# A two-layer trunk with a mixture of experts on one core: block pairs without tokens move to the front of the block table, and the first tokens are fetched ahead of the scatter

## The reference, condensed

```python
def hierarchical_moe(h, wg, bg, we, be, w1, w3, w2):
    x = h.reshape(b * t, d)
    pg_sel, g_sel = lax.top_k(softmax(x @ wg + bg), 1)          # one of 4 groups
    le = (x @ we + be).reshape(-1, N_GROUPS, EXPERTS_PER_GROUP)
    w_top, i_top = lax.top_k(softmax(le_sel), TOP_K)            # two of its 4 experts
    ...
    hid = silu(x @ w1[e]) * (x @ w3[e])
    y = sum over the two experts of gate * (hid @ w2[e])
```

## Time and profile before

| | |
|---|---|
| median of 3 runs | 2230.29 us (2224.9 to 2230.62) |
| profiled execution: its time / its span | 2219.47 us / 2217.3 us |
| busy: PE, DVE, ACT, POOL | 1915.4, 896.2, 481.3, 373.1 us |
| mean granted TensorE clock | 0.918 of 2.4 GHz |
| pair loop, layer 0 (first L986 to last DVE copy) | 893.9 to 1083.7 us |
| pair loop, layer 1 | 1941.5 to 2149.4 us |

### The profile page before, as it was taken

The page is one execution under the profiler, slowest core; times in us unless marked ns, Lnnn a source line. Parts: engine busy times, 40 slices in busy tenths (PEclk is TensorE's granted clock), DMA queues, the critical chain, the costliest instruction groups (busy, mean ns, idle before and its releaser), DMA issues. The chain is left out here.

```text
span 2217.3 us, 24642 instructions
## 1 busy us (share of the span) xinstructions
PE 1915.4 (86%) x9669; PEld 1300.0 (59%) x9669; DVE 896.2 (40%) x1686; ACT 481.3 (22%) x810; POOL 373.1 (17%) x280
## 2 busy tenths in 40 slices
PE   3899978978888895899679999888888889599975
PEld 2455655558888754444345566556888865444433
DVE  2179014565555424011237920546555541311114
ACT  1211013351111213122131101344111120322212
POOL 0001150043433102100111000005444300300001
PEclk8999897999999997899789999899999999699996
DMA  9322896800000003999562112530000000499953
GB/s 358 41 75 82 278 290 209 298 1 1 1 1 1 10 2 129 354 364 365 218 161 76 38 57 77 197 126 1 1 1 1 1 12 0 168 383 358 372 226 121
DMA packets 113920, 302.54 MB, mean 136 GB/s; under 512 B 27904, under 2 KB 35746, under 8 KB 100642
## 3 DMA queue, kind: packets, MB, share of 16 engines
q1 hardware_dynamic: 65424, 218.73, 26.7%
q0 software_dynamic: 14080, 53.48, 7.3%
q10 hardware_dynamic: 34322, 28.99, 4.6%
HBM read 235.09 MB, written 67.05 MB: 136 GB/s over the span
## 5 line engine op out<-in xcount | busy, mean ns | idle before, releaser
L626 PE MATMUL ps<-hreg,ring 128*128 128x512 f32 x768 | 400.2, 603 | 7.7 <-ACT hreg L1141 7.7
L627 PEld LDWEIGHTS ps<-hreg,ring 128*128 128x128 f32 x768 | 147.8, 192 | 187.6 <-issue 187.6
L986 PE MATMUL ps<-ring,tok 128*128 128x512 f32 x544 | 237.9, 595 | 0.2 <-issue 0.2
L986 PEld LDWEIGHTS ps<-ring,tok 128*128 128x128 f32 x544 | 103.9, 191 | 130.9 <-issue 130.9
L627 PE MATMUL ps<-hreg,ring 128*128 128x128 f32 x768 | 149.0, 276 | 0.0
L1969 POOL TENSOR_TENSOR hreg<-hreg,cst 128x512 f32<-128x512 f32 x70 | 88.9, 1270 | 301.7 <-DVE hreg L1674 254.7
L1001 PE MATMUL ps<-ring,work 128*128 128x512 f32 x272 | 123.7, 598 | 0.0
L626 PEld LDWEIGHTS ps<-hreg,ring 128*128 128x128 f32 x768 | 118.8, 195 | 8.0 <-issue 8.0
L1881 DVE TENSOR_TENSOR work<-work,ps 128x256 f32<-128x256 f32 x34 | 14.2, 421 | 252.5 <-ACT work L1364 252.5
L1503 DVE SCALAR_TENSOR_TENSOR mixA<-cin_reg,small,mixA 128x655 f32<-128x655 f32 x120 | 107.0, 895 | 0.0
L1687 DVE TENSOR_TENSOR hreg<-hreg,ps 128x512 f32<-128x512 f32 x50 | 34.3, 687 | 164.9 <-PE ps L846 164.9
(11 more groups left out here) (358 smaller groups left out, 3306.5 us busy)
## 6 DMA issues: line engine op xcount, KB each, us to landing
ring<-in_w SPq DMA_DIRECT2D x102, 1024.0 KB, 8.2
ring<-in_w_mod SPq DMA_DIRECT2D x24, 2048.0 KB, 8.6
ring<-in_w_in SPq DMA_DIRECT2D x12, 2048.0 KB, 9.0
ys<-zs ACTq DMA_DIRECT2D x34, 512.0 KB, 7.8
tok<-xs SPq DMA_DIRECT2D x30, 512.0 KB, 11.0
xs<-zero POOLq DMA_DIRECT2D x8, 1792.0 KB, 19.6
ys<-zero POOLq DMA_DIRECT2D x8, 1664.0 KB, 18.6
ring<-in_w_out SPq DMA_DIRECT2D x4, 2048.0 KB, 8.1
```

Source lines behind the costliest of these rows:

```text
L626: mm(o[:, 0:TS], lhs(k), rhs(k)[:, 0:TS], start=k == 0, stop=k == nk - 1)
L627: ins = mm(o[:, TS:T], lhs(k), rhs(k)[:, TS:T], start=k == 0, stop=k == nk - 1)
L986: ins = mm(bank(2 + q), xgT[q][:, k, :], w, start=k == 0, stop=k == KD - 1)
```

## The change

The diff makes seven edits. On POOL the fetches for blocks 2 and 3 move ahead of the ten scatters. On PE the second `turn_block` writes another part of PSUM (columns 2048 on) and no longer waits for ACT's first copy; ACT copies from there. SP waits for the second fetch (`xf_loaded[1]`) before it starts the weights of block 1. The bias matmuls L939 are gone: two small matmuls in the output projection (m == 2) spread the bias row over partitions, DVE keeps it in `crb`, and adds it where it copied the logits. DVE norms rows 0 to 3 right after `lrow`, POOL rows 4 to 7, and ACT takes the rows in order; DVE's late `norm_one(1)` after the routing is gone. Unused pairs come first: `skip` (unused blocks) is added to the block numbers, `skip` times 128 to `slots`, and `blocks` gets three more entries; slots are written later on DVE, behind the hot rows. And the branch of each loop turns round: pairs below `unused` only raise counters. Not shown below: the ACT and DVE loops, which turn round as PE's does, with the same counters raised as before, and declarations.

```diff
@@ -516,15 +517,22 @@
                     need(ht_copied, c_ + 1)
                     sp.dma_start(hx[P * c_:P * (c_ + 1), :], htok[:, c_, :]).then_inc(hx_stored.sem, 16)
                 need(blocks_ready, 1)
+                need(xf_loaded[1], 16)
                 sp.sem_inc(once["turns"], 1)
-                e = sp.value_load(blocks[0:1, 1:2], min_val=0, max_val=NE - 1)
+                e = sp.value_load(blocks[0:1, NBLK + 2:NBLK + 3], min_val=0, max_val=NE - 1)
                 up_load(1, e)
                 down_load(1, e)
                 need(xs_written, 16 * 2 * NCH)
-                in_use = sp.value_load(blocks[0:1, NBLK:NBLK + 1], min_val=1, max_val=NBLK)
+                unused = sp.value_load(blocks[0:1, NBLK + 1:NBLK + 2], min_val=2, max_val=NBLK + 2)
                 experts = {}
                 with sp.Fori(1, NPAIR) as pr:
-                    with sp.If(pr * 2 < in_use):
+                    with sp.If(pr * 2 < unused):
+                        for q in range(2):
+                            sp.sem_inc(ring_loaded[q], 32)
+                            sp.sem_inc(w2_loaded[q].sem, 16)
+                            sp.sem_inc(xg_loaded[q].sem, 16)
+                    with sp.Else():
+
                         for q in range(2):
                             e = sp.value_load(blocks[0:1, bass.ds(pr * 2 + q, 1)], min_val=0, max_val=NE - 1)
                             experts[q] = e
@@ -536,15 +544,6 @@
                             xg_load(q, pr * 2 + q + 2)
                             sp.wait_ge(y_done.sem, y_done.at(l, q - 1) + pr * 2)
                             down_load(q, experts[q])
-                    with sp.Else():
-
-                        for q in range(2):
-                            sp.wait_ge(ring_loaded[q], up_base[l][q] + pr * 32)
-                            sp.sem_inc(ring_loaded[q], 32)
-                            sp.wait_ge(w2_loaded[q].sem, w2_loaded[q].at(l, 0) + pr * 16)
-                            sp.sem_inc(w2_loaded[q].sem, 16)
-                            sp.wait_ge(xg_loaded[q].sem, xg_loaded[q].at(l, -16) + pr * 16)
-                            sp.sem_inc(xg_loaded[q].sem, 16)
 
             sp.wait_ge(once["y_stored"], 32)
 
...
@@ -916,6 +915,12 @@
                         for k in range(KD):
                             ins = mm(ps[0:2, 2900:2920], mod[:, 24 + k, :], wr[:, k, :], start=k == 0, stop=k == KD - 1)
                         ins.then_inc(logit_rows.sem, 1)
+                    if m == 2:
+                        need(logit_copied, 1)
+                        for g_ in range(2):
+                            ins = mm(ps[:, 2940 + 20 * g_:2960 + 20 * g_], ident[0:2, g_:g_ + 1].to_broadcast([2, P]), crow,
+                                     start=True, stop=True)
+                        ins.then_inc(logit_rows.sem, 1)
 
                 need(mod2_ready, 2)
@@ -934,9 +939,7 @@
                 need(route_loaded, 16)
                 for t in range(NCH):
                     o = ps[:, 2048 + 20 * t:2068 + 20 * t]
-                    g_ = 0 if t < TS // P else 1
-                    mm(o, lrow[:, P * t:P * (t + 1)], route_c[:, X_SEL:X_SEL + 20], start=True, stop=False)
-                    ins = mm(o, ident[0:2, g_:g_ + 1].to_broadcast([2, P]), crow, start=False, stop=True)
+                    ins = mm(o, lrow[:, P * t:P * (t + 1)], route_c[:, X_SEL:X_SEL + 20], start=True, stop=True)
                 ins.then_inc(logits.sem, 1)
 
                 need(sel_ready, 1)
...
@@ -1021,21 +1024,19 @@
                 need(slots_ready, 1)
                 need(xf_loaded[0], 16)
                 turn_block(0)
-                need(xg_copied, 1)
                 need(xf_loaded[1], 16)
-                turn_block(1)
+                turn_block(1, 2048)
                 need(blocks_ready, 1)
                 pe.sem_inc(once["turns"], 1)
-                in_use = pe.value_load(blocks[0:1, NBLK:NBLK + 1], min_val=1, max_val=NBLK)
+                unused = pe.value_load(blocks[0:1, NBLK:NBLK + 1], min_val=0, max_val=NBLK)
                 with pe.Fori(0, NPAIR) as pr:
-                    with pe.If(pr * 2 < in_use):
-                        pair(pr)
-                    with pe.Else():
-
+                    with pe.If(pr * 2 < unused):
                         for sig, n in ((up_done, 0), (xg_turned, 2), (hid_turned, 0), (y_done, 0)):
                             pe.wait_ge(sig.sem, sig.at(l, n) + pr * 2)
                             pe.sem_inc(sig.sem, 2)
-
+                    with pe.Else():
+
+                        pair(pr)
 
                 need(xg_copied, NBLK + 2)
                 for c_ in range(NCH):
...
@@ -1350,9 +1351,9 @@
                 def wait(pr, sig, base, step):
                     act.wait_ge(sig.sem, sig.at(l, base) + pr * step)
 
-                def copy_tokens(pr, q):
+                def copy_tokens(pr, q, a=0):
                     wait(pr, xg_turned, q + 1, 2)
-                    A_(xgT[q], ps[:, 0:D].rearrange("p (k n) -> p k n", k=KD), ACT.Copy).then_inc(xg_copied.sem, 1)
+                    A_(xgT[q], ps[:, a:a + D].rearrange("p (k n) -> p k n", k=KD), ACT.Copy).then_inc(xg_copied.sem, 1)
 
                 def store(pr, q):
                     wait(pr, y_out, q + 1, 2)
...
@@ -1761,13 +1763,18 @@
                     if m == 1:
                         need(logit_rows, 1)
                         V.tensor_tensor(crow, ps[0:2, 2900:2920], rbias[0:2, :], ALU.add).then_inc(logit_copied.sem, 1)
+                    if m == 3:
+                        need(logit_rows, 2)
+                        V.tensor_copy(crb[:, 0:4, :], ps[:, 2940:2960].rearrange("p (a n) -> p a n", a=1).to_broadcast([P, 4, 20]))
+                        step(V.tensor_copy(crb[:, 4, :], ps[:, 2960:2980]))
                     if m >= 2:
                         add_square(m - 1)
                 add_square(KD - 1)
                 need(norm_r, 2)
-                need(logit_rows, 2)
+                need(logit_rows, 3)
                 V.tensor_tensor(lrow, ps[:, 3072:3072 + T], rst, ALU.mult).then_inc(logit_copied.sem, 1)
-                norm_one(0)
+                for k in range(4):
+                    norm_one(k)
 
                 def r(a, n):
                     return rt[:, a:a + NCH * n].rearrange("p (c n) -> p c n", c=NCH)
@@ -1789,7 +1796,7 @@
                     step(V.tensor_tensor(out, ci, wide(mn, 4), ALU.is_equal))
 
                 need(logits, 1)
-                step(V.tensor_copy(lr, ps[:, 2048:2148].rearrange("p (c n) -> p c n", c=NCH)))
+                step(V.tensor_tensor(lr, ps[:, 2048:2148].rearrange("p (c n) -> p c n", c=NCH), crb, ALU.add))
                 one_hot(og, lr[:, :, 0:4], mx)
                 V.tensor_tensor(e4, lr[:, :, 0:4], wide(mx, 4), ALU.subtract).then_inc(rt_in.sem, 1)
                 le = lr[:, :, 4:20].rearrange("p c (g e) -> p c g e", g=NG)
@@ -1813,11 +1820,9 @@
                 V.tensor_tensor(e16(oh[0]), ogw, spread(o1), ALU.mult)
                 step(V.tensor_tensor(e16(oh[1]), ogw, spread(o2), ALU.mult))
                 V.tensor_tensor(rt[:, 0:80], oh[0], oh[1], ALU.add).then_inc(sel_ready.sem, 1)
-                norm_one(1)
-
                 need(ranks, 1)
                 nb, off, end, pos = rsc[:, 160:176], rsc[:, 176:192], rsc[:, 192:208], rsc[:, 208:288]
-                pick, sl, bf, wide_ = rsc[:, 288:368], rsc[:, 368:378], rsc[:, 378:379 + NBLK], rsc[:, 410:410 + NBLK * NE]
+                pick, sl, bf, wide_ = rsc[:, 288:368], rsc[:, 368:378], rsc[:, 378:381 + NBLK], rsc[:, 410:410 + NBLK * NE]
 
                 def last_bc(ap, n):
                     return ap.rearrange("p (e a) -> p e a", a=1).to_broadcast([P, ap.shape[-1], n])
...
@@ -1842,7 +1847,6 @@
                 for i in range(2):
                     step(V.tensor_tensor(pick, pos, oh[i], ALU.mult))
                     step(V.tensor_reduce(sl[:, NCH * i:NCH * (i + 1)], pick.rearrange("p (c e) -> p c e", c=NCH), AX, ALU.add))
-                V.tensor_copy(slots[:, :], sl).then_inc(slots_ready.sem, 1)
                 row_, base_ = rsc[:, 880:890], rsc[:, 890:900]
                 hb = rsc[:, 900:940].rearrange("p (n b) -> p n b", n=2 * NCH)
                 step(V.tensor_tensor(hb, last_bc(sl, 4), mid_bc(cst[:, C_THR + 1:C_THR + 5], 2 * NCH), ALU.is_ge))
@@ -1852,11 +1856,22 @@
                 step(V.tensor_tensor(hb, last_bc(base_, 4), mid_bc(cst[:, C_IOTA:C_IOTA + 4], 2 * NCH), ALU.is_equal))
                 V.tensor_tensor(hot_blk, hb, last_bc(route_c[:, X_TOK:X_TOK + 2 * NCH], 4), ALU.mult).then_inc(sel_ready.sem, 1)
 
+                t3 = wide_[:, 0:NPAIR]
+                used, skip = rsc[:, 940:941], bf[:, NBLK:NBLK + 1]
+                step(V.tensor_tensor(t3, end[:, NE - 1:NE].to_broadcast([P, NPAIR]),
+                                     cst[:, C_BLK:C_BLK + NBLK].rearrange("p (n a) -> p a n", a=2)[:, 0, :], ALU.is_gt))
+                step(V.tensor_reduce(used, t3, AX, ALU.add))
```

(18 more changed lines are left out.)

39 lines of the change are left out of this document (20 added, 19 removed).

## The result

The changed kernel takes 2268.5 us (median of 4 runs, 2265.91 to 2271.16) against 2230.16 us before: a ratio of 1.0179, 95% interval 1.0158 to 1.0200, some 38 us slower. The forecast was 2253 us, at most 2263: direction and mechanism held, the size did not. The profiled run took 2265.91 us, its span is 2264.0 us.

The account below looks back on a forecast made before the run. PE was taken to bound the pair loop, so only its entry and exits count: weights' counters behind the scatter +30.6 us, exits -7.5, sum +23.1, giving 2253 us on the median; range 2236 to 2263 us.

Parts of the forecast that it names:

- the sign that I had named: At PE's loop entry: each layer's first `up` starts 5 to 6 us behind the end of SP's scatter wait.
- The exits: At the pair loops' ends: POOL's gather goes on when the last store lands; 4.4 and 3.1 us gained, together -7.5 us.
- Rival 3: At loop entry: scatter doesn't hold PE, ACT's copies and rounds do (904.9 and 1937.1); -5.6 us, 2225 us; chance 0.10.
- when the scatter lands: Ahead of the pair loop: landing at 906.5 and 1953.3, against SP's earlier wait ends of 903.4 and 1951.0.
- my own sum of bytes: Weights, fetches and scatter ahead of the loop: 9.44 MB at 389 GB/s, 24.3 us, ending at 907.0 and 1953.8.
- near the bytes: Scatter landing put at 906.5 and 1953.3, between POOL's floor (903.5 and 1950.3) and the byte sum (907.0 and 1953.8).
- Rival 1: Ahead of the loop: scatter lands at POOL's pace, 903.5 and 1950.3; 6 us less, 2247 us; chance 0.17.
- The first fetch: Behind norm and routing: fetch by index starts 3.9 us earlier in each layer, at 875.6 and 1922.4.
- The four norm rows on DVE: Second norm, beside POOL's four: 1.5 us a row, 6 us counted, ending at 855.1 in layer 0.
- rival 2: Second norm: POOL and DVE in strict turns, 9.6 us instead of 6, 3.5 us a layer; +30 us, 2260; chance 0.11.
- Layer 0's first pair: Start of layer 0's loop: parameter loads run while PE waits, so the pair costs 23.8 instead of 28.5 us, -4.7.
- The bias: Output projection: bias matmuls and `crb`, two tiny operations each a layer, listed under nothing gained or lost.

Follow-up runs that it names:

- e1: Changed kernel with SP's wait for the scatter moved from ahead of its loop into the used pairs, where token rows are read; 2240.28 us, 1.0057 of before.
- e3: Changed kernel with both edits: SP's scatter wait in the used pairs, ACT's parameter loads behind the pair loop; 2221.67 us, 0.998 of before.
- e5: Kernel before with the new block numbering alone (table, slots, order of the rounds); 2253.77 us, 1.0112 of before.
- e9: Changed kernel without SP's wait for the second fetch, so block 1's weights are issued early; 2260.57 us, 1.0137 of before.
- e8: e7 with all eight rows of the second norm on DVE, none on POOL; 2213.61 us, 0.9937 of before.
- e7: e3 with each engine's unused rounds in a loop of their own, ahead of its work for the first block; 2217.22 us, 0.994 of before.
- e2: Changed kernel with ACT's 17 parameter loads for the next layer behind its pair loop instead of ahead; 2266.45 us, 1.0171 of before.
- e11: e8 without SP's wait for the second fetch; 2208.35 us, 0.9913 of before.

## Why the prediction was right in direction and wrong in size

**Right.** The first `up` begins 5.7 and 3.8 us behind the end of SP's wait (forecast 6.0 and 4.8; the sign that I had named was 5 to 6, so layer 1 lies under it); e1 and e3 show that the wait is the cause. The exits gave 4.4 and 3.1 us to the tenth, and their releaser is a landing. Rival 3 (the scatter doesn't hold PE) fell with that.

**The term that was mis-sized most: when the scatter lands.** I forecast it 3.1 and 2.3 us later than before; from the mark it is 9.1 and 5.4 later (58.07 to 67.22, 59.63 to 65.02): 6.0 and 3.1 us of error. The weights were issued 1.4 and 0.2 us later than forecast, the rest is my rate: 9.44 MB at 389 GB/s were to take 24.3 us, and took 28.4 and 26.7; and I had put the landing 0.5 us under my own sum of bytes. The transfers of layer 1 from about the weights' issue to the landing in 40 slices, first of the changed kernel and then of e5, whose order is that of before:

```profile
GB/s 0 196 245 430 466 393 380 387 417 350 368 344 362 338 338 258 344 331 387 411 399 423 442 399 411 430 436 399 423 442 405 405 430 442 393 417 436 209 80 12
```

```profile
GB/s 376 154 296 345 407 407 468 419 419 394 388 499 370 407 253 253 246 345 407 413 431 413 431 407 425 413 431 419 419 400 431 437 413 394 407 419 388 376 407 413
```

The middle is as full as ever. Without its first and last three slices the changed stretch moves 8.96 MB in 22.7 us, 395 GB/s. But it starts from idle transfers and runs dry at its end, where in the old order other transfers were under way at both ends; the six slices at the ends hold 0.5 MB, 1.3 us' worth, in 4.0 us. In layer 0 the same ends hold 0.4 MB in 4.3 us, and the middle moves 385 GB/s, 0.26 MB of it parameters. The step "near the bytes, because the same bytes filled both stretches of before" took a mean from the middle of a queue for the time from an empty queue to its last byte. Rival 1 (the pace of POOL, earlier) fell too; e9 shows that pace only where the weights are gone.

**A hold that I priced too low: ACT in layer 0.** Rival 3 let ACT through at 904.9, from loads of 14.5 us. They took 24.4 (888.48 to 912.88, `in_w_in` alone 10.69), and the last counter of its rounds rises at 919.7. Had the scatter landed as forecast, layer 0's first `up` would have come 67.2 us behind the mark by SP and not before 71.4 by ACT (e1), so that 4.2 of the layer's 5.7 us of error would have stayed.

**Smaller terms.** The first fetch was to come 3.9 us earlier in each layer; it came 2.7 and 3.8. The four norm rows on DVE took 7.74 us; I had counted 6, the strict turns of rival 2 came to 9.6. POOL's rows in the kernel before (layer 0, durations in ns):

```profile
L2002 POOL TENSOR_TENSOR hreg<-xT,rst x6: 1528/1530/2119, 848.3 to 856.4; 128x640 f32<-128x640 f32 x6
```

The third of them, at 851.90, ran while DVE stood idle (between 850.53 and 853.58), so a row takes POOL 1.53 us alone, and DVE 0.82 (e8); such rows start 1.49 and 0.74 us apart. In the changed kernel, side by side, a row of each goes by every 2.07 us, where strict turns would make 2.23 and no sharing 1.49. The Trainium skill's page "SBUF — State Buffer", section "SBUF: two separate sides", is the rule behind rival 2; here the trace comes close to it, with 2.07 us of the 2.23. Layer 0's first pair was to give back 4.7 us and gave 2.9, and layer 1's, put at nothing, cost 1.3: PE starts at the lower clock, where e7 and e8 start at the full one. The bias, put at nothing, is four passes in PE's own time, 0.62 us a layer; from the output projection's first matmul on `mixA` to the mark it is 72.94 us before (layer 0) and 73.68 now (layer 1), both at a granted 1.00, so 0.74 us a layer:

```profile
801.69 0.62 PE L921 MATMUL ps<-work,cst 2*128 2x20 f32 x4
```

**The sum.** First `up` +5.7 and +2.1 over forecast (the late landing, less the 0.3 and 1.0 us by which SP's rounds were shorter than I had put them), first pairs +3.1, bias +1.5, exits none: 12.4 us over +23.1 is +35.5, of the measured 38. The remaining 3 us are within the spread of the runs.

**What stays open.** Whether ACT's parameter loads slow the scatter at all: e2 moved the entry by no more than such entries differ by themselves. And why the granted clock behind like idle times (29.8 and 31.7 us in e2) is 0.50 in one layer and 0.69 in the other; no run takes that apart.

## What to carry to other kernels

Work that is moved ahead of a loop does not only leave the end: it meets every wait that stands there, so ask of each engine which wait its counters are queued behind, and put each wait where its data is read (with e1 and e2 together the loss of 38 us is gone). Where two engines hold the same instruction, undoing either shows almost nothing; undo both. A mean rate read from the middle of a full queue is not the time of a burst: add its empty start and its end.

## What the runs showed of the hardware

- Eight rows of 128x640 took 5.96 us on DVE alone; four beside POOL's four took 7.74 us. Alone a row took 0.82 us on DVE and 1.53 on POOL; side by side a row of each went by every 2.07 us.
- In the 5 us behind the first `up` PE's granted clock was 1.00 in e7 and e8, 0.70 and 0.66 in e11 (3.7 and 4.3 us of waiting between the two turned blocks), and 0.50 to 0.71 behind 13 to 33 us of idle PE (eleven cases).
- A wait of 3.6 us in e7's loop cost more than its length: the turn and the `down` behind it took 1.97 and 5.36 us in place of 1.05 and 3.60, at a granted 0.87.
- A 128x512 matmul on 32-bit numbers is two passes of 0.43 us in PE's rows at the full clock.
- A scatter of 512 KB landed 12.6 us behind its issue beside 3 MB of weights and 6.4 us with those out of the way.
